# Chunk inverses of the RWKV-7 recurrence: 128-column block matrices tile by tile, or 64-column matrices on two diagonal quarters of the array, level by level

## What is computed

```python
def _rwkv_scan(r, w, k, v, kk, a, s0):
    def step(s, inp):
        r_t, w_t, k_t, v_t, kk_t, a_t = inp
        s_kk = jnp.einsum('bhvk,bhk->bhv', s, kk_t)
        s = s * w_t[:, :, None, :] - s_kk[..., None] * (kk_t * a_t)[:, :, None, :] + v_t[..., None] * k_t[:, :, None, :]
        return s, jnp.einsum('bhvk,bhk->bhv', s, r_t)
```

## Time and profile before

| | us |
|---|---|
| median of the runs | 3956.7 (3954.9 to 3963.9) |
| the profiled execution | 3967.4 |
| its span in the profile | 3965.1 |
| inverse stage of layer 1, from the first L1525 to the first L1577 | 771.3 to 937.0 |
| inverse stage of layer 2 | 2744.1 to 2909.9 |

### The profile page before, as it was taken

How to read it: one execution, slowest core, us unless ns; L and a number is a source line. 1 busy time by engine, 2 the same in 40 slices (tenths; PEclk the granted TensorE clock), 3 DMA queues, 4 the chain that set the end, 5 groups by cost and what they waited for, 6 DMA issues and landing times. The chain is left out here.

```text
span 3965.1 us, 70246 instructions
## 1 busy us (share of the span) xinstructions
PE 3009.2 (76%) x30196; PEld 2060.5 (52%) x30196; DVE 1393.5 (35%) x2867; ACT 570.9 (14%) x1054; POOL 836.3 (21%) x998
## 2 busy tenths in 40 slices
PE   4998856298667888889559988563986578988883
PEld 0554546197335556655315645452973355665562
DVE  1103677644442111112410036876454421112114
ACT  0102320321110010000100033203211101000011
POOL 0003555463110000000100044644721100000002
PEclk9998978599878999999779989776998789999996
DMA  7300000000416877887163000000004077788771
GB/s 312 119 11 31 1 10 1 6 1 1 154 48 232 299 287 274 295 293 277 60 276 109 6 32 1 10 1 6 1 1 177 30 262 289 282 302 292 278 286 48
DMA packets 134696, 535.47 MB, mean 135 GB/s; under 512 B 12704, under 2 KB 14688, under 8 KB 130656
## 3 DMA queue, kind: packets, MB, share of 16 engines
q1 hardware_dynamic: 131104, 519.41, 35.7%
q0 software_dynamic: 3264, 11.14, 1.0%
HBM read 521.74 MB, written 8.78 MB: 134 GB/s over the span
## 5 line engine op out<-in xcount | busy, mean ns | idle before, releaser
L2218 PE MATMUL ps<-arena 128*64 128x80 f32 x16384 | 627.7, 239 | 157.0 <-issue 152.4
L2218 PEld LDWEIGHTS ps<-arena 128*64 128x64 f32 x16384 | 610.0, 142 | 193.0 <-issue 191.5
L2237 PE MATMUL ps<-arena 128*128 128x512 f32 (+1 forms) x1024 | 446.3, 594 | 1.9
L2302 DVE TENSOR_TENSOR arena<-arena,ps 128x32 f32<-128x32 f32 (+1 forms) x192 | 45.2, 263 | 1098.9 <-ACT arena L2251 1098.9
L2237 PEld LDWEIGHTS ps<-arena 128*128 128x128 f32 (+1 forms) x1024 | 172.8, 170 | 261.5 <-issue 257.1
L492 PE MATMUL ps<-arena 128*128 128x128 f32 (+1 forms) x1088 | 296.4, 435 | 5.3 <-DVE arena L545 5.3
L2171 POOL COPY arena<-arena 80x1 uint32 x32 | 16.9, 527 | 1179.7 <-DVEq L2281 1051.7
L492 PEld LDWEIGHTS ps<-arena 128*128 128x128 f32 x1088 | 164.8, 192 | 137.0 <-issue 131.2
L420 PE MATMUL ps<-arena,scT 128*2 128x512 f32 x384 | 97.0, 664 | 125.9 <-DMA arena<-in_ada_w 125.8
L1449 POOL TENSOR_TENSOR arena<-arena,hgm_sb 128x512 f32<-128x512 f32 x140 | 161.7, 1183 | 137.0 <-PE ps L1550 77.6
L1932 PE MATMUL ps<-arena 128*128 128x512 f32 x320 | 142.3, 608 | 25.5 <-DMA arena<-in_w_out 25.5
(11 more groups left out here) (336 smaller groups left out, 4622.5 us busy)
## 6 DMA issues: line engine op xcount, KB each, us to landing
arena<-in_ex_w SPq DMA_DIRECT2D x128, 2048.0 KB, 10.9
arena<-in_ex_w SPq DMA_DIRECT2D x128, 1024.0 KB, 5.2
arena<-in_ada_w SPq DMA_DIRECT2D x24, 2048.0 KB, 18.8
arena<-in_w_t SPq DMA_DIRECT2D x34, 512.0 KB, 3.6
arena<-in_w_out SPq DMA_DIRECT2D x4, 2048.0 KB, 10.2
arena<-in_w_tok SPq DMA_DIRECT2D x2, 3712.0 KB, 16.8
h_d<-x_sb SPq DMA_DIRECT2D x10, 512.0 KB, 2.6
arena<-mod_d SPq DMA_DIRECT2D x8, 512.0 KB, 8.4
```

Source lines behind the costliest of these rows:

```text
L2218: m = nc.tensor.matmul(gated(j)[c * 64:(c + 1) * 64, f, a, :], w13[:, j, a, k, f * P + c * 64:f * P + (c + 1) * 64], xT[:, b, k, :], start ...
L2237: m = nc.tensor.matmul(ps[0:CAP if b == 0 else P, 4 + h, :], r[:, f, :], w2[:, (f // 2 + 2) % 4, f % 2, h * 512:(h + 1) * 512], start=f == ...
L2302: m = nc.vector.tensor_tensor(rows[b][:, 2 * j:2 * j + 2, to:to + c1 - c0], hs[:, j % 2, :, c0:c1], gated(j)[:, :, 1, c0:c1], ALU.mult)
```

## The change

The inverses are held as 64-column matrices. The two chunks of a tile lie in partitions 0 to 63 and 64 to 127, so each matmul uses 64 rows and 64 columns of the array: rows and columns 0 to 63 for the one chunk (`LO`), 64 to 127 for the other (`HI`), both into one bank, in different partitions. `products` makes the factor and its transpose directly, by two products with swapped operands, so `turn` is gone. The order is level by level: a level over all five tiles, then the next. One group now holds both directions: 16 small matmuls, one ACT copy, one or two DVE subtractions of 128x512. PE issues `inner(n)` ahead of `outer(n-1)`. The constants `hgm` and `bds` give way to a smaller `rwl`, with the signs in it; the DVE makes X's and Y's starts, POOL the level masks and Y's identity. The scan reads the same inverses from their new places. In the diff the pieces stand in the order ACT, POOL, PE, DVE.

```diff
-                sp.dma_start(hgm[:, :, :].rearrange("p a b -> p (a b)"), d["hgm"]).then_inc(S["ld_const"], 16)
+                sp.dma_start(rwl[:, :, :].rearrange("p a b -> p (a b)"), d["rwl"]).then_inc(S["ld_const"], 16)
                 sp.dma_start(rwm[:, :, :].rearrange("p a b -> p (a b)"), d["rwm"]).then_inc(S["ld_const"], 16)
-                sp.dma_start(bds[:, :, :].rearrange("p a b -> p (a b)"), d["bds"]).then_inc(S["ld_const"], 16)
...
+    def product(par, w):
+        return ps[:, (2 if w else 6) + par, 0:4 * C].rearrange("p (l a n) -> p l a n", l=2, a=2)
+    def eight(b):
+        return ps[:, b, :].rearrange("p (l h n) -> p l h n", l=2, h=HH)
...
+            def factors(t):
+                act.wait_ge(S["pr_ps"], 4 * t + 4)
+                for par in range(2):
+                    nc.scalar.activation(raw[:, t, :, 2 * par:2 * par + 2, :], product(par, 1), ACT.Copy).then_inc(S["m_ev"], 1)
+            factors(0)
+            factors(1)
+            for n in range(LVC * TILES):
+                act.wait_ge(S["t1_ps"], 2 * n + 2)
+                if n >= 2:
+                    act.wait_ge(S["dxy_ps"], 2 * n - 2)
+                nc.scalar.activation(T1[:, n % 2], eight(4 + n % 2), ACT.Copy).then_inc(S["t1_sb"], 1)
+                if n + 2 < TILES:
+                    factors(n + 2)
...
+            for n in range(LVC * TILES):
+                j, t = divmod(n, TILES)
+                if j == 0:
+                    pool.wait_ge(S["m_ev"], 2 * t + 2)
+                if n >= 4:
+                    pool.wait_ge(S["t1_ps"], 2 * (n - 4) + 2)
+                nc.gpsimd.tensor_tensor(Mj[:, n % 4], raw[:, t], e.rwl[:, :, j + 2:j + 3, :].to_broadcast([P, 2, HH, C]), ALU.mult
+                                        ).then_inc(S["mj"], 1)
+                if j == 0:
+                    pool.wait_ge(S["y0m"], t + 1)
+                    nc.gpsimd.tensor_tensor(Yst[:, t], Yst[:, t], unit, ALU.add).then_inc(S["y0"], 1)
...
+                    pe.wait_ge(S["m_ev"], 2 * t)
+                    pe.wait_ge(S["l_ev"], t)
+                for w in range(2):
+                    for dp in range(4):
+                        for cpar, rows in enumerate((LO, HI)):
+                            c = 2 * t + cpar
+                            for par, r in enumerate((LO, HI)):
+                                keys, reads = KB[r, dp, c, 1, :], AR[r, dp, 0, ck(c)]
+                                m = nc.tensor.matmul(ps[rows, (2 if w else 6) + par, dp * C:(dp + 1) * C], keys if w else reads,
+                                                     reads if w else keys, start=True, stop=True)
...
+            def inner(n):
+                j, t = divmod(n, TILES)
+                if j == 0:
+                    pe.wait_ge(S["x0"], t + 1)
+                else:
+                    pe.wait_ge(S["xy"], n - TILES + 1)
+                if n >= 2:
+                    pe.wait_ge(S["t1_sb"], n - 1)
+                pe.wait_ge(S["mj"], n + 1)
+                for u in range(2 * HH):
+                    ln, h = divmod(u, HH)
+                    for r in (LO, HI):
+                        m = nc.tensor.matmul(ps[r, 4 + n % 2, u * C:(u + 1) * C], Mj[r, n % 4, ln, h, :], X[r, t, ln, h, :],
+                                             start=True, stop=True)
...
+            def outer(n):
+                j, t = divmod(n, TILES)
+                if j == 0:
+                    pe.wait_ge(S["y0"], t + 1)
+                pe.wait_ge(S["t1_sb"], n + 1)
+                if j < LVC - 1:
+                    if n:
+                        pe.wait_ge(S["xu"], n)
+                    for u in range(2 * HH):
+                        ln, h = divmod(u, HH)
+                        for r in (LO, HI):
+                            m = nc.tensor.matmul(ps[r, 0, u * C:(u + 1) * C], Yst[r, t, ln, h, :], T1[r, n % 2, ln, h, :],
+                                                 start=True, stop=True)
...
+                if n:
+                    pe.wait_ge(S["xy"], n)
+                for u in range(2 * HH):
+                    ln, h = divmod(u, HH)
+                    for r in (LO, HI):
+                        m = nc.tensor.matmul(ps[r, 1, u * C:(u + 1) * C], T1[r, n % 2, ln, h, :], Yst[r, t, ln, h, :],
+                                             start=True, stop=True)
...
             products(0)
+            for n in range(LVC * TILES):
+                if n + 1 < TILES:
+                    products(n + 1)
+                inner(n)
+                if n:
+                    outer(n - 1)
+            outer(LVC * TILES - 1)
...
+            def pairs(t):
+                dve.wait_ge(S["pr_ps"], 4 * t + 4)
+                for par in range(2):
+                    v.add(nc.vector.tensor_tensor(X[:, t, :, 2 * par:2 * par + 2, :], product(par, 0),
+                                                  e.rwl[:, :, 7:8, :].to_broadcast([P, 2, 2, C]), ALU.mult))
                 v.join()
+                dve.sem_inc(S["l_ev"], 1)
+                dve.wait_ge(S["m_ev"], 2 * t + 2)
+                nc.vector.tensor_tensor(Yst[:, t], raw[:, t], e.rwl[:, :, 1:2, :].to_broadcast([P, 2, HH, C]), ALU.mult
+                                        ).then_inc(S["y0m"], 1)
+                nc.vector.tensor_tensor(X[:, t], X[:, t], unit, ALU.add).then_inc(S["x0"], 1)
+            def update(n):
+                j, t = divmod(n, TILES)
+                if j < LVC - 1:
+                    dve.wait_ge(S["dx_ps"], 2 * n + 2)
+                    nc.vector.tensor_tensor(X[:, t], X[:, t], eight(0), ALU.subtract).then_inc(S["xu"], 1)
+                dve.wait_ge(S["dxy_ps"], 2 * n + 2)
+                nc.vector.tensor_tensor(Yst[:, t], Yst[:, t], eight(1), ALU.subtract).then_inc(S["xy"], 1)
+            pairs(0)
+            pairs(1)
+            for n in range(LVC * TILES):
+                update(n)
+                if n + 2 < TILES:
+                    pairs(n + 2)
```

More of the change, by code:

```diff
@@ L50 @@
 LV = 7
+LVR = 8
 ALPHA = float((2 * DEPTH) ** 0.25)
@@ L75, in constants @@
         m[1, j + 1] = m[0, j + 1].T
-    hgm = m.transpose(2, 0, 1, 3).reshape(P, 2 * (LV + 1) * P)
+    rwl = np.zeros((P, 2, LVR, C), np.float32)
+    for dr in range(2):
+        for half in range(2):
+            q = slice(half * C, (half + 1) * C)
+            rwl[q, dr, 0:7] = m[dr, 0:7, q, q].transpose(1, 0, 2)
+            rwl[q, dr, 1] *= -1
+            rwl[q, dr, 7] = -m[1 - dr, 1, q, q]
     far = [[i[(i % (2 << j) >= 1 << j) != (d == 1)] for j in range(LV)] for d in range(2)]
@@ L212, in program @@
         ident = sb("ident_sb", [P, P])
-        hgm = sb("hgm_sb", [P, 2, (LV + 1) * P])
+        rwl = sb("rwl_sb", [P, 2, LVR * C])
         rwm = sb("rwm_sb", [P, 2, P])
-        bds = sb("bds_sb", [P, 2, P])
         blk = sb("blk_sb", [P, P])
@@ L1279, in phase_rwkv @@
     yst0 = z
-    Yst, z = e.part(z, 2, TILES, HH, P)
+    Yst, z = e.part(z, TILES, 2, HH, C)
+    Mj, z = e.part(z, 4, 2, HH, C)
     sq, _ = e.part(yst0, NCH * HH * HD, rows=C)
[L1283 to L1286, removed]
+    raw, z1 = e.part(e.a0, TILES, 2, HH, C)
+    T1, z1 = e.part(z1, 2, 2, HH, C)
     assert z1 <= e.a1
@@ L1290, in phase_rwkv @@
     assert z1 <= e.a1
-    x0, z1 = e.part(e.a1, 2, HH, P)
-    T1, z1 = e.part(z1, 2, HH, P)
+    X, z1 = e.part(e.a1, TILES, 2, HH, C)
+    assert z1 <= e.a1 + 4 * PAD
     ys, z1 = e.part(e.a1, NCH, HH * HD, rows=C)
     assert z1 <= e.a1 + 4 * PAD
-    x1, z = e.part(z, 2, HH, P)
-    X = (x0, x1)
     mid, z = e.part(z, 4, NCH)
@@ L1311, in phase_rwkv @@
     LVC = 5
+    unit = e.rwl[:, :, 0:1, :].to_broadcast([P, 2, HH, C])
+    def product(par, w):
+        return ps[:, (2 if w else 6) + par, 0:4 * C].rearrange("p (l a n) -> p l a n", l=2, a=2)
+    def eight(b):
+        return ps[:, b, :].rearrange("p (l h n) -> p l h n", l=2, h=HH)
     def blockrow(c):
@@ L1521, in products @@
                 if t:
-                    pe.wait_ge(S["mt_sb"], 2 * t)
-                for dp in range(4):
-                    for par, r in enumerate((LO, HI)):
-                        m = nc.tensor.matmul(ps[:, 6 + par, dp * P:(dp + 1) * P],
-                                             AR[r, dp, 0, t * P:(t + 1) * P], KB[r, dp, 2 * t:2 * t + 2, 1, :], start=True, stop=True)
-                        if dp == 3:
-                            m.then_inc(S["l_ps"], 1)
-            def turn(t):
-                pe.wait_ge(S["ls"], t + 1)
-                for ln in range(2):
-                    for h in range(HH):
-                        m = nc.tensor.transpose(ps[:, 6 + ln, h * P:(h + 1) * P], Ls[:, ln, h, :], e.ident[:, :])
-                    m.then_inc(S["mt_ps"], 1)
@@ new lines, in products @@
+                    pe.wait_ge(S["m_ev"], 2 * t)
[8 more added lines that the diff above has]
+                                                     reads if w else keys, start=True, stop=True)
+                                if w and dp == 3:
+                                    m.then_inc(S["pr_ps"], 1)
```

118 lines of the change are left out of this document (18 added, 100 removed).

## The result

The changed kernel takes 3686.0 us in the median (3666.3 to 3689.9), the kernel before 3960.3 us in runs on the same chip (3954.9 to 3963.9): a ratio of 0.929, with an interval of 0.927 to 0.932.

What follows compares the result with a forecast made beforehand. PE was taken to bound the inverse stage: 74.2 us work plus 14.0 waits gives 88.2 instead of 165.7 us. Both layers save 155.0, constants 2: 3956.7 - 157 = 3799.7, say 3800 us, range 3780 to 3842.

Steps and rivals of the forecast that it cites:

- the stage: Inverse stage of each layer: 88.2 us instead of 165.7, a gain of 77.5 us a layer.
- Pace: Inverse stage, PE's work: 2560 records a layer at 29 ns each, 74.2 us; bounds 28 and 34 ns.
- Waits: Inverse stage, PE waiting: 1.0 us before products(1), 3.6 before products(3) and (4), 3.1 before inner(4), 1.1 at the end.
- DVE beside POOL: Inverse stage, level 0: DVE and POOL both working from SBUF add 1.5 us, bounds 0 and 6.
- The clock: Start of the inverse stage: products(0) and products(1) at half speed on a cold clock, 3.7 us more.
- Constants: First 18 us of the kernel: 0.66 MB less to load, saving 2 us, bounds 0 and 2.5.
- A: Inverse stage: two quarters writing one bank don't run together, 59 ns a record, about 3955 us, no change; chance 6%.
- B: Inverse stage: changing quarter also costs time, 70 ns a record, 193.2 us a layer, 4010 us in all; chance 3%.
- D: Inverse stage: clock stays at its lower level because half the array works, 155 us, 3934 us in all; chance 4%.
- C: Inverse stage: instructions don't come fast enough, PE stops after each 128 records, 135 us, 3893 us in all; chance 5%.
- cost of all these: nothing: Other engines' work and edits, such as POOL's, DVE's and ACT's, cost nothing while PE has 88 us in the inverse stage.

Runs made afterwards that it cites:

- e1: Kernel before with 21 tiny matmuls (84 PE instructions) added in the modulation's PE program, which moves all later PE code: 3843.3 us, ratio 0.970.
- e9: Kernel before with each load of expert weights from the second expert on cut to 16 KB: 3746.9 us, against 3958.0 beside it.
- e12: Changed kernel with each load of expert weights from the second expert on cut to 16 KB: 3586.5 us.
- e4: Changed kernel with all LO matmuls before all HI ones in the inner and both outer loops, instead of alternating: 3937.0 us.
- e3: Changed kernel with the constants' old sizes in HBM and unused SBUF tiles, so every tensor has its old address: 3678.8 us, ratio 0.928.
- e5: Changed kernel with pairs(n+2) put ahead of update(n) in DVE's order: 3666.7 us, ratio 0.926.

## Why the prediction was right and wrong

**Right: the stage.** 88.2 us forecast, 87.0 and 87.2 measured.
- Pace: 29 ns, taken from matmuls that shared rows or columns, measured 29 ns in diagonal quarters. The products were not 29 but 14.5 ns a record: all four quarters of the array alternate there, and four records start 7, 7, 8 and 36 ns apart. The sum had 13.0 us for the five `products`, the cold clock included; they took 1.99 + 1.99 + 1.96 + 1.16 + 1.16 = 8.3 us.
- Waits: before products(1) 1.15 (1.0), before products(3) and (4) 1.63 each (1.8 each), before inner(4) 2.92 (3.1), at the end 0.88 (1.1): 0.6 us less than forecast together. The 0.88 us before the last Y part and 0.13 us twice behind products the sum didn't have.
- DVE beside POOL: the first L1745 took 1.68 us and the second L1747 1.76, 1.0 us longer each than the others. But only the first held PE up, by 0.29 us before inner(0), so the term of 1.5 us was 1.2 us too large.
- The clock: the granted clock rose at 776.7 us, 9.1 us into the stage. The sum had products(0) and (1) at half speed; inner(0) and products(2) were so too. It fell again for 3.4 us behind the wait before inner(4), which the sum didn't have. In inner(0), inner(4) and the X part behind it this cost some 2 us.
- Constants: 1.8 us (2).

So the stage's sum is right within 1.2 us in part by luck: terms that were 6.5 us too large (products, contention, waits) stand against some 3 us that it lacked (clock, small waits) and 2 us more that aren't traced one by one. The pace, which makes 65 of the 87 us, is no luck.

e1 and the changed kernel have their experts' code at the same place; they differ by 3843.3 - 3686.0 = 157.3 us. That is the forecast gain, and e9 and e12 give 160.4.

**Right: the rivals against the stage.** A, B and D would have shown 59 ns or more, or a clock of 0.50. In the kernel as it stands none came. e4 shows they were real: a single quarter gives 107 ns, and its stage of 209 us is beyond the 193 us of rival B. Against the stage of before e4 loses 2 x 43 us; that its total is still below 3963 comes from the experts' new place. The rule of the Trainium skill, TensorEngine Tiling (Array Packing), "Gotcha 1: PSUM Pressure", which the prediction weighed for rival A, doesn't hold here by the letter: the two quarters of a pair write one bank in different partitions and start 3 to 4 ns apart. C didn't come either: 20 packets of instructions landed in the stage and PE never stopped for one.

```profile
q8 instruction: 20, 0.33, 1.5%
```

**Wrong: the step from the stage to the time.** The sum subtracted the stage's gain from the whole and put "cost of all these: nothing" on everything else. That supposes that code which isn't touched takes the same time as before. The experts' stage, at which the sum had 0, took 137 us less in the profiled executions; by the medians the whole forecast was 274 - 157 = 117 us off. The mechanism was in view: rival C read from the earlier trace rows that PE stops after each 128 records while the weights stream and doesn't while DMA is idle, and the page of before put 152.4 us of idle time in front of L2218 down to "issue". The rival asked only what this would do to the inverse stage. It didn't ask what the change does to the stage where those stops are: a change of PE's instruction count ahead of a loop moves the loop's block borders, with either sign. A range that had allowed for it would have needed some 100 us more at its lower end. The trace of before had the waits, some 5 us at each turn of the loop among them, but not which of them another place would spare: that the place of before was a bad one shows only beside others.

## What to carry to other kernels

Where "issue" stands in front of an engine's main group while DMA is busy, look whether packets of instructions land just before the engine goes on. In this kernel that was time lost on code loading, and how much depended on where the loop lay in the code; an edit ahead of it moved the kernel by 3%, so compare stage by stage, and judge such an edit beside a version with the loop put back at its old place. A few useless matmuls are a cheap way to try places. Small matmuls that use one quarter of the array each ran fast here when they alternated between quarters, in diagonal pairs (29 ns a record) or all four (14.5 ns), and slowly one quarter at a time (84 ns).

## What the hardware showed unasked

- Matmuls on one quarter at a time ran at a granted clock of 0.50 throughout the stage of e4, 107 ns a record within a quarter; in diagonal pairs a record takes 29 ns and the clock is up.
- Four alternating quarters take 58 ns for four records, as long as two take in a diagonal pair.
- PE's code and the weights compete: the same expert stage took 613 to 617 us with the DMA engines at 0.07, and 654 to 726 us with them at 0.76 to 0.83, by the place of its code.
- Even one place isn't sharp: the experts of layer 1 took 654 to 665 us in kernels with the same expert code at the same place (after, e1, e3, e4, e5), with 16 to 40 us of both layers at the lower clock. It may be what spreads the runs of the changed kernel from 3666 to 3690 us; only one of them was profiled, so this isn't shown.
